# Beginning four output items instead of two inside the last unit of both attentions

## The reference

```
o = lax.map(block, jnp.arange(s // Q_BLOCK))      # softmax attention, 16 heads of 64
return _merge_blocks(o) @ w_out                   # "fox" attention, output product
...
o = o * lax.rsqrt(jnp.mean(jnp.square(o), axis=-1, keepdims=True) + RMS_EPS_2)
o = (o * subln_g.astype(jnp.float32) * (1.0 - lambda_init)).astype(x.dtype)
return _merge_blocks(o) @ w_out                   # "diff" attention, output product
...
x = _layer_norm(DN_ALPHA * x + h, ln_attn_g[layer], ln_attn_b[layer])
```

## Time and profile before

| | us |
|---|---|
| median of 3 runs | 1912.71 (1911.44 to 1914.56) |
| the profiled execution, its time | 1913.45 |
| its span, first to last instruction | 1911.7 |
| TensorE busy | 1838.3 (96%) |
| VectorE busy | 770.8 (40%) |
| GpSimd busy | 1036.9 (54%) |

### The profile page before, as it was taken

The page is one execution under the profiler, slowest core; times in us unless marked ns, Lnnn a source line. Parts: engine busy times, 40 slices in busy tenths (PEclk is TensorE's granted clock), DMA queues, the critical chain, the costliest instruction groups (busy, mean ns, idle before and its releaser), DMA issues.

```text
span 1911.7 us, 27221 instructions
## 1 busy us (share of the span) xinstructions
PE 1838.3 (96%) x8911; PEld 1532.0 (80%) x8911; DVE 770.8 (40%) x1387; ACT 781.7 (41%) x1638; POOL 1036.9 (54%) x937
## 2 busy tenths in 40 slices
PE   6999999999999999899999999889998999999997
PEld 5878888888887787788888888878786888888887
DVE  6955000001125455564333322456655643333224
ACT  4433323332234555345444422445654354444223
POOL 5846656555562222356666655465554566666651
PEclk8989999999999999999999999899999899999998
DMA  4303333323334444223333233333232233332331
GB/s 126 98 9 89 95 103 88 99 85 104 86 87 108 122 115 108 80 69 97 97 89 99 86 105 85 78 77 83 68 81 66 67 93 95 98 99 85 99 91 67
DMA packets 328500, 170.90 MB, mean 89 GB/s; under 512 B 43426, under 2 KB 318964, under 8 KB 328436
## 3 DMA queue, kind: packets, MB, share of 16 engines
q1 hardware_dynamic: 327026, 169.49, 32.0%
q10 hardware_dynamic: 1410, 0.59, 0.1%
HBM read 151.10 MB, written 2.10 MB: 80 GB/s over the span
## 4 chain that ended last, share of the span: by engine, by line
PE 80%; ACT 4%; DVE 4%; POOL 3%; issue 3%; DMA 3%; SPq 3%; ACTq 0%; DVEq 0%; POOLq 0%
PE bank L875 23%; PE bank L877 22%; PE bank L876 22%; PE attended L875 2%; PE attended L876 2%; PE attended L877 2%; SPq L639 2%; DMA raw<-in_kv_w 1%; DVE xres L1868 1%; POOL WL L675 1%; PE turned L1211 1%; POOL XL L708 1%; DVE small L2021 1%; ACT pmap L1581 1%; ACT XH L1420 1%
## 5 line engine op out<-in xcount | busy, mean ns | idle before, releaser
L675 POOL TENSOR_TENSOR WL<-raw,WH 128x512 fp32r<-128x512 f32 (+3 forms) x656 | 787.0, 1223 | 618.2 <-ACT WH L1370 617.3
L875 PE MATMUL bank<-XL,WH 128*128 128x512 f32 x1456 | 581.2, 399 | 13.1 <-ACT work L1596 5.6
L877 PE MATMUL bank<-XH,WL 128*128 128x512 f32 x1456 | 569.2, 391 | 0.0
L876 PE MATMUL bank<-XH,WH 128*128 128x512 f32 x1456 | 568.2, 390 | 0.0
L1370 ACT ACTIVATE WH<-raw 128x512 fp32r<-128x512 f32 (+3 forms) x656 | 338.4, 566 | 351.2 <-PE bank L877 203.9
L875 PEld LDWEIGHTS bank<-XL,WH 128*128 128x128 f32 x1456 | 275.8, 189 | 68.2 <-issue 8.6
L877 PEld LDWEIGHTS bank<-XH,WL 128*128 128x128 f32 x1456 | 275.1, 189 | 58.3
L876 PEld LDWEIGHTS bank<-XH,WH 128*128 128x128 f32 x1456 | 275.9, 190 | 52.0
L877 PE MATMUL bank<-HH,WL 128*128 128x512 f32 (+1 forms) x528 | 201.1, 381 | 0.0
L876 PE MATMUL bank<-HH,WH 128*128 128x512 f32 (+1 forms) x528 | 201.1, 381 | 0.0
L875 PE MATMUL bank<-HL,WH 128*128 128x512 f32 (+1 forms) x528 | 201.0, 381 | 0.0
(11 more groups left out here) (276 smaller groups left out, 2597.9 us busy)
## 6 DMA issues: line engine op xcount, KB each, us to landing
raw<-in_ffn_w_in SPq DMA_DIRECT2D x88, 512.0 KB, 3.8
raw<-in_w_gate SPq DMA_DIRECT2D x22, 512.0 KB, 3.8
raw<-in_w_up SPq DMA_DIRECT2D x22, 512.0 KB, 3.8
raw<-in_ffn_w_out SPq DMA_DIRECT2D x28, 384.0 KB, 3.4
raw<-in_ffn_w_out SPq DMA_DIRECT2D x28, 320.0 KB, 3.1
raw<-in_a_w_in SPq DMA_DIRECT2D x16, 512.0 KB, 4.1
raw<-in_kv_w SPq DMA_DIRECT2D x32, 256.0 KB, 4.0
raw<-in_w_in SPq DMA_DIRECT2D x12, 512.0 KB, 3.8
```

The lines of the kernel that those rows point to most:

```text
L675: pool.tensor_tensor(wl, x, wh, ALU.subtract).then_inc(w_lo, 1)
L875: pe.matmul(out_, wh, xl, start=start, stop=False)
L876: pe.matmul(out_, wh, xh, start=False, stop=False)
L877: return pe.matmul(out_, wl, xh, start=False, stop=stop)
```

## The change

In both last units 28 steps are woven in instead of 14: items 0 and 1 up to k-tile 6, one after the other, and then items 2 and 3, up to k-tile 6, in the two score banks, which are free once the last scores have been read. The last k-tile of all four items follows the last unit's output. In diff a 13th slot is added, which holds `mean_square`, with four steps behind it. ScalarE and GpSimd split the weights of items 2 and 3 in the places of the unit where the next unit's v weights were split. `stage` begins at item 4; VectorE takes tiles 2 and 3 from the score banks.

```diff
+            MOST = [(j, k) for j in range(2) for k in range(DT - 2)] + [(0, DT - 2), (1, DT - 2)] + \
+                [(j, k) for j in (2, 3) for k in range(DT - 1)]
+            REST = [(j, DT - 1) for j in range(4)]
...
-                for k in ks:
+                for j, k in pairs:
                     ready(k)
-                    for j in range(2):
-                        if k == 0:
-                            bank_free(Nth(u + j))
-                        step(Nth(g + j), (u + j) % 2, OH, OL, 0, k, DT, True, True)
-                        yield
+                    if k == 0 and j < 2:
+                        bank_free(Nth(u + j))
+                    if k == 0 and j >= 2:
+                        pe.wait_ge(ex[j - 2], scored + OPEN)
+                    step(Nth(g + j), j if j < 2 else 2 + j, OH, OL, 0, k, DT, True, True)
+                    yield
...
-                    weave(out_steps("out1", ready, range(DT - 1)), fox_slot(au), (0,) * 3 + (2,) * 9)
-                    for _ in out_steps("out1", ready, [DT - 1]):
+                    weave(out_steps("out1", ready, MOST, scored), fox_slot(au), (1, 1, 2, 2, 2, 1, 2, 1, 2, 3, 3, 8))
+                    for _ in out_steps("out1", ready, REST, scored):
                         pass
...
-                    weave(out_steps("out2", ready, range(DT - 1)), diff_slot(au), (0,) * 5 + (2,) * 7)
-                    mean_square(au)
-                    for _ in out_steps("out2", ready, [DT - 1]):
+                    weave(out_steps("out2", ready, MOST, scored), diff_slot(au), (1, 1, 2, 2, 2, 1, 2, 1, 2, 3, 4, 3, 4))
+                    for _ in out_steps("out2", ready, REST, scored):
                         pass
...
+                if fed:
+                    bank_free(u + -2)
+                elif not apart:
                     bank_free(u)
...
-                for j in range(2, DT - 2):
-                    whole(name, j, per=DT, x=(hi, lo))
+                for j in range(2 if name == "out" else 4, DT - 2):
+                    whole(name, j, per=DT, x=(hi, lo), fed=name != "out")
...
+                    if iu is None and sl in SLOT_OF_ITEM[:2]:
+                        high(Nth(STAGES["out1"][0] + 2 + SLOT_OF_ITEM.index(sl)))
...
-                with own.loop(DT // 2 - 1, (2 if centred else 1) * 2) as it:
-                    for j in range(2):
-                        tile(it, j)
+                if name in ("out1", "out2"):
+                    for t in range(DT - 2):
+                        tile(t // 2, t % 2, sc if t // 2 == 1 else bank)
```

More of the change, by code:

```diff
@@ L303, in two_blocks @@
         halves_of = [bank, ob]
-        banks = bank + ob
+        banks = bank + ob + sc
         y_bank = [ob[0], bank[0], bank[1], ob[1], sc[0], sc[1], ob[0], bank[0]]
@@ L809, in _ @@
                     low(Nth(STAGES["qkv1"][0] + j + 2, it, 4), (UNIT[2:] + UNIT[:2])[j])
-            lows("out1")
+            for i in range(2, DT + 2):
+                low(Nth(STAGES["out1"][0] + i))
             lows_of_halves(3, "gu1")
@@ L850, in unit_lows @@
                     return
-                if iu is not None:
+                if iu is None:
+                    low(Nth(STAGES["out2"][0] + 2))
+                else:
                     next_low(iu, 0)
@@ L854, in unit_lows @@
                     sub_low(au + -1)
-                if iu is not None:
+                if iu is None:
+                    low(Nth(STAGES["out2"][0] + 3))
+                else:
                     next_low(iu, 1)
@@ L865, in _ @@
             sub_low(Nth(UNITS - 1))
-            lows("out2")
+            for i in range(4, DT + 2):
+                low(Nth(STAGES["out2"][0] + i))
             lows_of_halves(5, "gu2")
@@ L913, in two_items, with whole @@
                             mm.then_inc(item_done, 1)
-            def whole(name, j, it=0, per=4, x=(XH, XL), apart=False):
+            def whole(name, j, it=0, per=4, x=(XH, XL), apart=False, fed=False):
                 u = Nth(STAGES[name][1] + j, it, per)
-                if not apart:
+                if fed:
+                    bank_free(u + -2)
+                elif not apart:
                     bank_free(u)
@@ L1273, in ready @@
                             pe.wait_ge(o_read[e], k + 1 + OPEN)
-                    weave(out_steps("out1", ready, range(DT - 1)), fox_slot(au), (0,) * 3 + (2,) * 9)
-                    for _ in out_steps("out1", ready, [DT - 1]):
+                    scored = 4 * UNITS
+                    weave(out_steps("out1", ready, MOST, scored), fox_slot(au), (1, 1, 2, 2, 2, 1, 2, 1, 2, 3, 3, 8))
+                    for _ in out_steps("out1", ready, REST, scored):
                         pass
@@ L1316, in work_of @@
                         attend(0, slot, u + UNITS)
+                    if sl == 12:
+                        mean_square(u)
                 return work_of
@@ L1329, in ready @@
                         pe.wait_ge(sub_lo, k + 1 + OPEN)
-                    weave(out_steps("out2", ready, range(DT - 1)), diff_slot(au), (0,) * 5 + (2,) * 7)
-                    mean_square(au)
-                    for _ in out_steps("out2", ready, [DT - 1]):
+                    scored = 2 * 4 * UNITS
+                    weave(out_steps("out2", ready, MOST, scored), diff_slot(au), (1, 1, 2, 2, 2, 1, 2, 1, 2, 3, 4, 3, 4))
+                    for _ in out_steps("out2", ready, REST, scored):
                         pass
@@ L1640, in _ @@
             weave_units(act.Fori, fox_part)
-            highs("out1")
+            for i in range(4, DT + 2):
+                high(Nth(STAGES["out1"][0] + i))
             warm(ACT.Sqrt)
@@ L1728, in diff_part @@
                         sub_high(before)
+                    if iu is None and sl in HIGH_AT[:2]:
+                        high(Nth(STAGES["out2"][0] + 2 + HIGH_AT.index(sl)))
                     if iu is not None:
@@ L1748, in _ @@
             sub_high(Nth(UNITS - 1))
-            highs("out2")
+            for i in range(4, DT + 2):
+                high(Nth(STAGES["out2"][0] + i))
             warm(ACT.Sqrt)
@@ L1965, in residual, with tile @@
                 centred = NORM[m] in CENTRED
-                def tile(it, j):
+                def tile(it, j, src=bank):
                     last = Nth(STAGES[name][0] + (j + 1) * items_of_tile - 1, it, 2 * items_of_tile)
@@ L1971, in tile @@
                     dve.wait_ge(item_done, last.n(1))
-                    dve.scalar_tensor_tensor(out=r, in0=r, scalar=factor, in1=bank[j][:, :].rearrange("p (a s) -> p a s", a=1),
+                    dve.scalar_tensor_tensor(out=r, in0=r, scalar=factor, in1=src[j][:, :].rearrange("p (a s) -> p a s", a=1),
                                              op0=ALU.mult, op1=ALU.add).then_inc(bank_read[j], 1)
@@ L1979, in tile @@
                     dve.tensor_tensor(ssq, ssq, tmp[0], ALU.add).then_inc(sum_tiles, 1)
-                with own.loop(DT // 2 - 1, (2 if centred else 1) * 2) as it:
-                    for j in range(2):
-                        tile(it, j)
+                if name in ("out1", "out2"):
+                    for t in range(DT - 2):
+                        tile(t // 2, t % 2, sc if t // 2 == 1 else bank)
+                else:
+                    with own.loop(DT // 2 - 1, (2 if centred else 1) * 2) as it:
+                        for j in range(2):
+                            tile(it, j)
                 if len(TAIL[name]) == 1:
```

2 lines of the change are left out of this document (1 added, 1 removed).

## The result

The changed kernel takes 1917.77 us (median of 8 runs, 1915.03 to 1920.51) against 1912.87 us (1911.44 to 1914.56, 8 runs on the same chip) for the kernel before: a ratio of 1.0022, 95% interval 1.0013 to 1.0032. It is slower, by 4.2 us as the ratio has it (4.9 by the two medians). The profiled execution took 1916.80 us, 3.35 more than the one of before.

A forecast was written before the change was run, and what follows sets the result against it. TensorE was busy for 96%, but with the change VectorE's residual tiles were to bound both stages: +1.4 us in fox and +2.3 in diff, +3.7 on the median of 1912.71, gave 1916.4; 8 in 10 range 1906.5 to 1922.

The forecast's parts named there:

- Fox, up to the last k-tiles: Fox unit: the last k-tiles begin at 806.4 instead of 802.78, after 14 more steps (+9.8) less filled waits and clock.
- the clock drop at 779: Fox unit: half-speed clock behind the 3.17 us wait, taken not to come, -2.7 us; with it 809.1.
- Four tiles 18.5 us: VectorE in `out1` and `out2`: the first four residual tiles take 18.5 us, bounds 14 and 22.
- Tile 4, 4.2 us: VectorE in both stages: residual tile 4 takes 4.2 us, after which `bank1` is free, in fox at 830.8.
- TensorE's wait: Fox stage: TensorE stands for 6 us before item 6's first half, until tile 4 frees `bank0` at 826.6.
- Clock in the stage, +0.8: Both stages: half speed in item 6 behind the `bank0` wait adds 0.8 us (0 to 2.5).
- Diff: Diff unit and `out2`: last k-tiles begin at 1476.9, VectorE at 1478.2, `half_stats` at 1508.2 against 1505.9, +2.3 us.
- Behind `half_stats` nothing has changed: Layer norms behind both stages: unchanged, so a shift of `half_stats` is carried to the end in full.
- TensorE stays the bound: Rival, both stages: residual tiles go fast enough, waits are simply saved, together -13.4 us, 1899; chance 0.08.
- The decision point of 3.2 us a tile: Both stages: TensorE stays the bound only if tile 4 starts within 13 us of tile 0, 3.2 us a tile.
- The argument for its small chance: Against TensorE staying the bound: only one of eight tiles in the two stretches was so fast (3.0 us).
- In between: Rival, both stages: low parts fall well, 14 us for four tiles and 3.5 for the next, about -7, 1906; chance 0.10.

The follow-up runs named there:

- single edits: Two kernels, the change made only in the fox attention or only in diff, against the kernel before: ratios 1.0015 and 1.0008.
- the fox part alone: Only the fox attention changed, diff left as in the kernel before: 1916.38 us, ratio 1.0015 against the kernel before.
- the diff part alone: Only the diff attention changed, fox left as in the kernel before: 1914.81 us, ratio 1.0008 against the kernel before.
- three kernels that make it real: Changed kernel with residual-tile sums and squaring cut to one column (0.9959), or sums in PSUM and squares on ScalarE, without (0.9953) or with score-bank halves (0.9951).
- the sums in PSUM: Changed kernel with the residual tiles' running sums kept in the two turned PSUM banks until tile 5: 1906.83 us, ratio 0.9963 against the kernel before.

## Why the prediction was right

The forecast was 1916.4 us, +3.7; measured are 1917.8, +4.2 by the ratio and +3.35 between the two profiled executions. The mechanism is the one forecast, and the experiments show it rather than make it likely. Its steps:

- *Fox, up to the last k-tiles*, 806.4 with the clock drop at 779 avoided. The drop was avoided. Tile 0 started at 808.55, not at 807.4: the forecast was 1.15 us too early; 0.7 of it are two waits of 0.25 and 0.46 us for the transposed maps, which I took as filled.
- *Four tiles 18.5 us*: 17.0 in fox, 16.85 in diff (1481.72 to 1498.57). Squarings of 1.8 and 0.7 us alternate tile by tile, so two tiles of 5.1 to 5.9 us go with two of 3.0. The term was mis-sized by 1.5 us, inside its bounds of 14 and 22; beside the four tiles ran 9 low parts in each stage, not 10 and 11.
- *Tile 4, 4.2 us*: 5.06 in both stages; it is one of the slow tiles. Six tiles are the thing to count, and there the errors cancel: forecast `bank1` free at 830.8, measured 831.3.
- *TensorE's wait*, 6 us: 4.2, as TensorE came 1.7 us later and the bank 0.3 earlier.
- *Clock in the stage, +0.8*: 0. Item 6 at half speed was done at 830.9, before `bank1` was free; 831.35 + 5.8 is 837.15 exactly. `half_stats` +1.2 against +1.4.
- *Diff*: unit 6's `attend`, ahead of the changed part, began 3.13 us late (1446.27 against 1443.14) and `half_stats` stood 4.28 late, so its own part is +1.15 against +2.3, less than forecast by about the 1.5 us of the four tiles. Both parts, +1.2 and +1.15, are hardly larger than the 1 us by which these times move from one execution to the next. By the single edits they are 2.9 us (1.1 to 4.6) in fox and 1.5 (-0.2 to 3.1) in diff: the signs stand, the split of 1.4 to 2.3 is not confirmed.
- *Behind `half_stats` nothing has changed*: this step failed. The norm took 31.9 us instead of 30.9 in fox, the clock falling at 840 rather than at 847, and 30.7 instead of 31.5 in diff. In fox this repeats: 31.6 in the fox part alone, 30.1 to 30.4 in the three other kernels with the old order and no delay. In diff it is the 31.5 of the profiled kernel before that stands out: three others with the old diff stage took 29.1, the diff part alone 30.5, so there too the norm is more likely longer with the change. By chance of that one execution the two nearly cancel here, and stages of +1.2 and +1.15 end as +3.4 with 0.9 us lost on the way between them, a stretch that moves by 1.1 us even among kernels with the old fox stage. The total is right to 0.5 us by the ratio and 1.4 by the median, with parts that are off by 1 to 1.5 each: the nearness of the total is in part luck.
- *The rivals*. "TensorE stays the bound" was put at -13.4; three kernels that make it real stand at -8 to -9.4. It put the stages at -7.0 and -6.4 us; in fox `half_stats` came 5.6 to 5.9 us early (830.1 to 830.3, forecast 829.0), in diff some 5 us of its own (1505.88 - 1496.39 = 9.5, less the 4.7 that the fox stage had brought). The norms then took 0.2 to 1.0 us each of it. The decision point of 3.2 us a tile (13 us for four) fits: at 14.45 us TensorE waited 1.6, at 8.0 not at all. The argument for its small chance, that only one tile in eight had been so fast, was weaker than it looked: in the changed kernel four of eight took 3.0 us, and the four tiles together still took 17. It is the sum that counts. "In between" (14 us for four tiles and 3.5 for the next: 1906) is what the sums in PSUM made real: 14.45 and 2.64 in fox, 15.14 and 2.85 in diff, and 1906.83.

What stays open is what sets the clock's moment inside the norm. All that is shown is that the norm's length varies between 29.1 and 34.9 us with the waits ahead of it and from one execution to the next.

## What to carry to other kernels

A change that fills the busiest engine's waits hands the stage to the engine next in line; count that engine's whole chain from its new start to the point that everything waits for, and forecast the time by whichever chain ends last. Two edits that are each worth nothing can be worth 7 us together, so when a promising reordering shows no gain, cut the next engine's work to one column in both kernels: two runs say at once whether it is the new bound and what freeing it would bring. Where VectorE and GpSimd work side by side, as here, one input in PSUM was a cheap way to keep them apart. And where a wait can't be avoided, look at what stands right behind it: the drop of the clock cost nothing ahead of item 6, which was done before its successor's bank was free, and 2.5 us ahead of the statistics.

## What the runs showed of the hardware

- Beside low parts a vector sum of 128 x 512 took 0.69 to 1.83 us with both inputs in SBUF, wherever its result went, and 0.69 to 0.70 us in every tile with one input in PSUM.
- Behind idle time of 3.93 us ahead of the statistics the granted clock was 0.50 for the next 7.7 us, and a lead of 2.9 us was gone by the end of the norm.
- Behind 1.62 us of idle time the clock stayed full, behind 4.20 and 5.75 it was at 0.5; in the stages with sums in PSUM waits of 1.6 and 2.52 us left it full too (1.00 from 826 to 834 and from 1492 to 1498).
